# Column projections in four pieces, norm biases folded into the transposes' copies, and two norms joined in a four-layer transformer kernel

## The reference

```python
for l in range(2):                                   # first block
    h = x @ w_in[l]                                  # 13 splits: fox, mla, stick, swa
    mix = concat(fox_attention, mla, stick_breaking, sliding_window)
    x = layernorm(ALPHA * x + group_rmsnorm(mix) @ w_o[l], ln1_g[l], ln1_b[l])
    f = (silu(x @ w_gate[l]) * (x @ w_up[l])) @ w_down[l]
    x = layernorm(ALPHA * x + f, ln2_g[l], ln2_b[l])
for l in range(2):                                   # second block
    x = x + 0.5 * swiglu(rms_norm(x, ffn_norm[l, 0]), ...)
    p = rms_norm(x, mix_norm[l]) @ w_in_2[l]
    x = x + concat(dsa_attention(p), rwkv7_time_mix(p), gated_deltanet(p)) @ w_out[l]
    x = x + 0.5 * swiglu(rms_norm(x, ffn_norm[l, 1]), ...)
```

## Time and profile before

| | |
|---|---|
| median of 3 runs | 4019.3 us (4017.92 to 4021.04) |
| the profiled execution | 4015.3 us |
| its span | 4013.4 us |
| granted TensorE clock, mean | 0.945 of 2.4 GHz |
| DMA | 292.37 MB, 73 GB/s mean |

### The profile page before, as it was taken

The page is one execution under the profiler, slowest core; times in us unless marked ns, Lnnn a source line. Parts: engine busy times, 40 slices in busy tenths (PEclk is TensorE's granted clock), DMA queues, the critical chain, the costliest instruction groups (busy, mean ns, idle before and its releaser), DMA issues.

```text
span 4013.4 us, 54320 instructions
## 1 busy us (share of the span) xinstructions
PE 3754.5 (94%) x23012; PEld 3097.8 (77%) x23012; DVE 1389.5 (35%) x2950; ACT 1407.8 (35%) x2393; POOL 1340.5 (33%) x639
## 2 busy tenths in 40 slices
PE   8987999998889989999998789999999999779999
PEld 7876888887678868888766678888888866668887
DVE  2345111334531232112775741112111486662111
ACT  2443222335332233223453433223222454434221
POOL 3103444430144443444320124444444320114443
PEclk9988999998799999999997899999999997889999
DMA  4101333320123332333210023333333320003332
GB/s 120 48 14 50 100 95 97 95 64 16 38 84 95 100 108 82 97 101 93 74 32 1 3 62 97 101 96 104 97 103 95 90 58 1 2 24 93 96 96 93
DMA packets 406785, 292.37 MB, mean 73 GB/s; under 512 B 18032, under 2 KB 356880, under 8 KB 406544
## 3 DMA queue, kind: packets, MB, share of 16 engines
q1 hardware_dynamic: 400976, 284.69, 23.8%
q10 hardware_dynamic: 5136, 2.96, 0.3%
q0 software_dynamic: 432, 1.25, 0.1%
HBM read 286.77 MB, written 2.10 MB: 72 GB/s over the span
## 4 chain that ended last, share of the span: by engine, by line
PE 53%; DVE 6%; ACT 3%; issue 1%; POOL 0%; ACTq 0%; DVEq 0%
PE ps L713 8%; PE ps L715 8%; PE ps L714 8%; PE ps L797 6%; PE ps L800 6%; PE ps L799 6%; PE ps L1316 2%; PE ps L740 1%; PE ps L851 1%; PE ps L742 1%; PE ps L741 1%; PE ps L868 1%; PE ps L1105 1%; PE ps L696 1%; PE ps L859 1%
## 5 line engine op out<-in xcount | busy, mean ns | idle before, releaser
L2892 POOL TENSOR_TENSOR wl<-wraw,wh 128x1024 fp32r<-128x1024 f32 (+2 forms) x532 | 1246.3, 2343 | 2258.7 <-ACT wh L2322 2258.6
L713 PE MATMUL ps<-x_T,wh 128*128 128x512 f32 (+1 forms) x2464 | 941.1, 382 | 18.2 <-POOL wl L2892 9.0
L714 PE MATMUL ps<-x_T,wh 128*128 128x512 f32 (+1 forms) x2464 | 936.9, 380 | 0.0
L715 PE MATMUL ps<-x_T,wl 128*128 128x512 f32 (+1 forms) x2464 | 936.6, 380 | 0.0
L2322 ACT ACTIVATE wh<-wraw 128x1024 fp32r<-128x1024 f32 (+2 forms) x532 | 548.7, 1032 | 1101.8 <-PE ps L800 593.9
L713 PEld LDWEIGHTS ps<-x_T,wh 128*128 128x128 f32 x2464 | 469.0, 190 | 108.2 <-issue 15.5
L715 PEld LDWEIGHTS ps<-x_T,wl 128*128 128x128 f32 x2464 | 468.7, 190 | 86.7
L714 PEld LDWEIGHTS ps<-x_T,wh 128*128 128x128 f32 x2464 | 469.0, 190 | 85.9 <-issue 0.5
L797 PE MATMUL ps<-wh,h_T 128*128 128x512 f32 x1056 | 411.4, 390 | 0.0
L800 PE MATMUL ps<-wh,h_T 128*128 128x512 f32 x1056 | 410.9, 389 | 0.0
L799 PE MATMUL ps<-wl,h_T 128*128 128x512 f32 x1056 | 410.8, 389 | 0.0
(11 more groups left out here) (712 smaller groups left out, 5132.2 us busy)
## 6 DMA issues: line engine op xcount, KB each, us to landing
wraw<-in_ffn_w_gate_dram SPq DMA_DIRECT2D x88, 512.0 KB, 3.8
wraw<-in_ffn_w_up_dram SPq DMA_DIRECT2D x88, 512.0 KB, 3.8
wraw<-in_w_in_dram SPq DMA_DIRECT2D x82, 512.0 KB, 3.8
wraw<-in_ffn_w_down_dram SPq DMA_DIRECT2D x80, 512.0 KB, 3.7
wraw<-in_w_gate_dram SPq DMA_DIRECT2D x44, 512.0 KB, 3.8
wraw<-in_w_up_dram SPq DMA_DIRECT2D x44, 512.0 KB, 3.8
wraw<-in_w_down_dram SPq DMA_DIRECT2D x40, 512.0 KB, 3.7
wraw<-in_w_o_dram SPq DMA_DIRECT2D x16, 512.0 KB, 3.7
```

Of the source, the lines that this page charges most:

```text
L713: mm(b[:, t0:t1], wh[:, k, :], xTh[:, k, t0:t1], k == 0, False)
L714: mm(b[:, t0:t1], wh[:, k, :], xTl[:, k, t0:t1], False, False)
L715: ins = mm(b[:, t0:t1], wl[:, k, :], xTh[:, k, t0:t1], False, k == 7)
L2892: tt(wl, raw_of(w), wh.bitcast(F32), ALU.subtract).then_inc(*g.sig("w", "lo", w))
```

## The change

1. **Mixer.** A column projection is cut into four pieces of two row blocks (6 matmuls) and not three; the project lane has 53 steps for 40, the heads rounds take four of them, and gates step every fourth round.
2. **Layer norms of the first block, but the joined one.** PE transposes what DVE's gain leaves, without the bias, two token tiles to a PSUM bank (`pair_T`). The bias, now per row block of the transposed x and so a column vector, is added by ACT as the bias of the copy (`high_pair`) and by DVE in the subtraction (`low_pair`), 8 instructions of 128x256 each per pair of tiles. POOL adds the bias to `xtm` later, one half tile in each of the first eight uses of the FFN (norm 2 of layer one: two in each of the first uses of layer two). DVE takes the reciprocal of tile 3 after the low parts of tiles 0 and 1.
3. **First projections.** `first_F` transposes tiles 0 and 1 before the halves and tiles 2 and 3 behind the first; its halves (`cols_half`) do the products with the high weight part first and wait for the low part only then. Behind the norms with pairs three projections are split, not two (`halves_F`). ACT and POOL stage the weights behind in another order. Norm 2 of layer one transposes its first two tiles within the last down projection.
4. **Joined norms.** DVE adds the bias itself, the squares, mean, root and scaling of a tile run two tiles behind (`behind_norm`), and the gain of rms norm (0, 0) is the scale of `high_pair` and an operand of `low_pair`; the L1556 multiplications of that norm and the row's DMA go.
5. **DMAs on ACT's queue.** The 12 row-vector DMAs go into the second group of the preceding FFN, the small projections' matrices (`lifts`) into that of the next.
6. **Squares.** ACT's four squares of q follow `index_heads`.

```diff
@@ project_lane, mixer_rounds
-    for t in range(40):
-        if t % 3 == 0 and t:
-            work(COLS2[t // 3 - 1])
-        if t < 39:
-            piece(COLS2[t // 3], t % 3)
+    for t in range(53):
+        if t % 4 == 0 and t:
+            work(COLS2[t // 4 - 1])
+        if t < 52:
+            piece(COLS2[t // 4], t % 4)
         yield
...
-        for _ in range(3):
+        for _ in range(4):
             next(project)
...
-            elif n % 3 == 0:
+            elif n % 4 == 0:
                 next(gates)
@@ PE
-                for k in ((0, 1, 2), (3, 4, 5), (6, 7))[n]:
+                for k in (2 * n, 2 * n + 1):
...
+            def halves_F(name, n, behind):
                 two = []
-                for n in range(2):
+                for m in range(n):
                     w = use()
                     b, free = bank(("F", w), ("ev", w))
                     pe.wait_ge(*free)
                     pe.wait_ge(*at("T", "lo", name, 1, 1))
-                    pe.wait_ge(*at("w", "lo", w))
-                    cols_F(w, b, 0, 2 * P)
+                    cols_half(w, b)
                     two.append((w, b))
-                    if n == 0:
-                        to_T(name, src, ready, (3,))
+                    if m == 0:
+                        behind()
...
+            def first_F(name, src, ready, done=()):
+
+                to_T(name, src, ready, [j for j in (0, 1) if j not in done])
+                halves_F(name, 2, lambda: to_T(name, src, ready, (2, 3)))
+
+            def pair_T(name, src, ready, j):
+
+
+                p = j // 2
+                if j % 2 == 0:
+                    for m in range(4):
+                        pe.wait_ge(*bank(("T", name, p, m), ("T", "b", name, p, m))[1])
+                for m in range(4):
+                    pe.wait_ge(*at(*ready(j, m // 2)))
+                    for e_ in range(2):
+                        o = (2 * e_ + j % 2) * P
+                        ins = tr(psum[book.bank[("T", name, p, m)]][:, o:o + P],
+                                 src[:, j, (2 * m + e_) * P:(2 * m + e_ + 1) * P])
+                    if j % 2:
+                        ins.then_inc(*pe.sig("T", "t", name, p, m))
...
+                halves_F(name, 3, behind)
@@ DVE
+            def low_pair(name, p, col, op):
...
+                        ins = stt(xTl[:, k, ts_], psum_of("T", name, p, m)[:, 2 * e_ * P:2 * e_ * P + 2 * P],
+                                  col[:, k:k + 1], xTh[:, k, ts_].bitcast(F32), op, ALU.subtract)
...
                 for i in range(NT + 1):
                     if i < NT:
                         close(i)
                         stats(i, 1)
                         mean(i)
-                        inverse(i)
+                        if last or i < 3:
+                            inverse(i)
                     if i:
                         gain(i - 1)
+                    if last and i:
+                        bias(i - 1)
+                    if last and 1 < i < NT:
+                        then(i - 2)
+                    if i == 3 and not last:
+                        low_pair(*pairs, 0, *cols_)
+                        inverse(i)
+                if last:
+                    low_pair(*pairs, 0, *cols_)
+                    then(2)
+                    then(3)
+                low_pair(*pairs, 1, *cols_)
@@ ACT
+            def high_pair(name, p, bias=None, scale=None):
...
+                        if bias is not None:
+                            ins = act(dst, src, ACT.Identity, bias=bias[:, k:k + 1])
+                        else:
+                            ins = act(dst, src, ACT.Identity, scale=scale[:, k:k + 1])
...
                 for i in range(NT):
                     if i == 3:
-                        stage(wat[0] + AHEAD)
+                        stage(wat[0] + 1)
+                        if not then:
+                            high_pair(name, 0, **cols_)
...
+                    if then and i > 1:
+                        then(i - 2)
+                if then:
+                    high_pair(name, 0, **cols_)
+                    then(2)
+                    then(3)
+                stage(wat[0] + AHEAD + 1)
+                high_pair(name, 1, **cols_)
...
+                index_heads(l)
                 for j in range(NT):
                     s.wait_ge(*at("ev", w, j))
                     act(scr[j][:, :], qtm2[:, j, :], ACT.Square).then_inc(*s.sig("dsa", "sq", l, j))
-                index_heads(l)
@@ POOL
+                stage(wat[0] + AHEAD + 1)
+                bias = layer_norm(l, 0)
+                for _ in range(62):
+                    use()
+                    next(bias, None)
                 use(6, True)
-                layer_norm(l, 1)
+                stage(wat[0] + AHEAD + 1)
```

More of the change, by code:

```diff
@@ L831, in early_T, with ffn @@
                     to_T(name, src, ready, (j - 1,))
-            def ffn(n, then=None):
+            def ffn(n, then=None, done=2):
                 for grp in range(2):
                     for f in range(11):
-                        if grp or f:
-                            proj_F()
-                            proj_F()
+                        for half in range(2):
+                            if grp or 2 * f + half >= done:
+                                proj_F()
                     for half in range(2):
@@ L1569, in rms_norm, with layer_norm @@
                 for i in range(NT):
[L1570 to L1571 removed]
+                    close(i)
                     gain(i, 1)
                     mean(i)
[L1574 removed]
+                    if 0 < i < 3:
                         low(name, i - 1)
                     inverse(i)
[L1577 removed]
+                for i in range(2, NT):
                     low(name, i)
[L1580 to L1582 removed]
+            def layer_norm(l, n, close, then=None):
                 def stats(i, half):
@@ L1608, in layer_norm @@
                 last = n == 1 and l == 1
+                pairs = [("rms", 0, 0) if last else (("ln1", "ln2")[n], l)]
+                cols_ = ((colat[("ffn_norm_2", 0, 0)], ALU.mult) if last else
+                         (colat[(("ln1_b", "ln2_b")[n], l)], ALU.add))
                 for i in range(NT + 1):
@@ L1640, in close @@
                             v.wait_ge(*at("w", *(("tile", w, j) if grp and half else ("used", w))))
+                            if base and not grp:
+                                v.wait_ge(*at(*base(j, half)))
                             finish(xtm[:, j, half * 512:(half + 1) * 512], grp,
@@ L1824, in close_o @@
                 v.wait_ge(*at("w", "tile", w, j))
+                if l and not g:
+                    v.wait_ge(*at("ln", "x", 0, 1, j, half))
                 stt(xs, xs, 1.0 if g else ALPHA, psum_of("Tm", w, j)[:, :], ALU.mult, ALU.add).then_inc(
@@ L2377, in norm, with behind_norm @@
                     act(rr, rr, ACT.Sqrt, bias=eps6).then_inc(*s.sig("rms", "root", l, n, i))
-                    s.wait_ge(*at("rms", "g", l, n, i, 1))
+                    if tiled:
+                        s.wait_ge(*at("rms", "g", l, n, i, 1))
                     s.wait_ge(*at("rms", "rr", l, n, i))
-                    act(mx[:, i, :], mx[:, i, :], ACT.Identity, scale=rr).then_inc(*s.sig("rms", "x", l, n, i))
-                tiled = (l, n) != (0, 0)
+                    act(mx[:, i, :], mx[:, i, :] if tiled else xtm[:, i, :], ACT.Identity, scale=rr).then_inc(*s.sig("rms", "x", l, n, i))
+                def behind_norm(i):
+                    square(i, 0)
+                    square(i, 1)
+                    norm(i)
+                if not tiled:
+                    return behind_norm
                 for i in range(NT):
@@ L2392, in rms_norm, with layer_norm @@
                 stage(wat[0] + AHEAD)
-                for i in range(2 if tiled else 0, NT):
+                for i in range(2, NT):
                     high(name, i)
-            def layer_norm(l, n):
-                name = ("ln1", l) if n == 0 else ("ln2", l)
+            def layer_norm(l, n, then=None):
                 s.preload_act_table(ACT.Sqrt)
+                name = ("rms", 0, 0) if then else (("ln1", "ln2")[n], l)
+                cols_ = {"scale": colat[("ffn_norm_2", 0, 0)]} if then else {"bias": colat[(("ln1_b", "ln2_b")[n], l)]}
                 for i in range(NT):
                     if i == 3:
-                        stage(wat[0] + AHEAD)
+                        stage(wat[0] + 1)
+                        if not then:
+                            high_pair(name, 0, **cols_)
                     rr = sml(42 + i)
@@ L2407, in layer_norm, with ffn @@
                         scale=rr[:, 0:1]).then_inc(*s.sig("ln", "n", l, n, i))
-                if not (n == 1 and l == 1):
-                    for i in range(NT):
-                        high(name, i)
-            def ffn(n):
+                    if then and i > 1:
[6 more added lines that the diff above has]
+                high_pair(name, 1, **cols_)
```

(20 more changed lines are left out.)

117 lines of the change are left out of this document (70 added, 47 removed).

## The result

The changed kernel takes 3974.2 us (median of 4 runs, 3970.44 to 3975.54) against 4018.8: a ratio of 0.9887, 95% interval 0.9869 to 0.9904. The forecast was 3990 with a range of 3968 to 4006. The profiled execution has a span of 3972.1 us, 41.3 less than before, where the sum had 29.5.

The account below looks back on a forecast made before the run. PE, busy 94% of the span, was taken to bound the kernel, gains coming where it waits or does unneeded work. Terms -5 - 10 - 5.5 - 1 - 4 - 4 = -29.5 gave span 3985.8, median 3990; range 3968 to 4006.

Parts of the forecast that it names:

- The norms: Layer norms of the first two layers: POOL's bias leaves the chain, 2.0 at norm 1 of each layer; sum 5.
- the joined norms: Joined norms of layer two: L1556 dropped, DMAs moved, bias on DVE, squares behind each bias; gain 10, bounds 8 and 13.
- first_F: First projections behind three rms norms: two tiles transposed first, high weight part first, so PE's waits fall; 5.5 in all.
- the wait of 19.1: PE's longest single wait for the scaled tiles of an rms norm (L2380), forecast to fall to about 12.
- The term for norm 2 of layer one: Second norm of layer one: halves start at 750.8 instead of 753.48, three projections done 1.0 to 1.5 earlier; taken as 1.0.
- Squares moved: Both mixers: PE gets L2624 2.2 us sooner with the squares behind index_heads; 2.0 each, 4.0, or 0 without cover.
- Mixers: Four pieces for three: early rounds -9, then +3, -9, +4, solve tail +8; taken as -2 for each mixer, -4.
- The rounds between: Mixer rounds 32 to 49 without the chain's costly steps, estimated -9; the steps put off fall on later rounds, +4.
- (1): Rival: mixers gain fully, early rounds keep 12.3 and the tail hides, -12 each instead of -2; 3970, chance 0.13.
- (2): Rival: the norms give half, short pieces and tile 3's late chain replacing PE's waits; 10 back, 4000, chance 0.2.
- (3): Rival: a thinner mixer chain keeps the low clock 17 us longer, +15 to +17 a mixer; at +17 4028, chance 0.08.
- (4): Rival: POOL's additions hold up DVE's in the FFN by the shared port; +36 if on the path, 4026, chance 0.04.

Follow-up runs that it names:

- b_rows: The kernel before with only its 12 row DMAs moved from the joined norms into the last FFN's second group: 4016.5 us against 4018.3, ratio 0.9999.
- a_hoist: The changed kernel with ACT staging the next weight ahead of the root for k, on which it waits for DVE: 3966.7 us, ratio 0.9873.
- a_squares: The changed kernel with part 6 undone, the squares back ahead of index_heads: 3973.0 us (6 runs), ratio 0.9907.
- a_hoist_sq: The changed kernel with the next weight staged ahead of the root for k and the squares back ahead of index_heads: 3983.0 us, ratio 0.9908.
- b_pieces: The kernel before with part 1 of the change alone, the four pieces: 4000.2 us against 4017.6, ratio 0.9955.
- b_late: The kernel before, still with three pieces, with the tiles' chain held back to round 41: 3995.1 us, ratio 0.9944.
- b_first: The kernel before with the new first_F alone, at all seven places: 4029.5 us (12 runs), ratio 1.0026.
- a_three: The changed kernel with part 1 undone, the project lane back in three pieces: 4013.3 us (12 runs) against 4017.6, ratio 0.9985.
- b_squares: The kernel before with part 6 alone, the squares behind index_heads: 4043.1 us (7 runs), ratio 1.0062.

## Why the prediction was right, and where not

**The norms, the joined norms and first_F** came as computed: -2.6, -2.6 and -10.5 for -2, -2 and -10, and -5.9 for -5.5. Each was read as a chain of single instructions up to the first half projection, then as PE work; the halves started within 0.5 us of the forecast times. One sign differs: the wait of 19.1 was to fall to about 12 and is now two of 5.0 and 5.8, since PE transposes one tile between them. The term for norm 2 of layer one was too high (-0.4 for -1). b_rows shows that of the causes I listed for the joined norms one, the row DMAs, counted for nothing.

**Squares moved, -4.** Wrong in sign. The step that failed: "What is late next is the DVE chain on q, by 1.9, with about 5 us in hand before its transposes". I looked at who reads q. The one who waited first was ACT's root for k, and what stood behind it on ACT's queue was a weight. a_hoist takes the weight out of that queue and gains 8.9; a_squares and a_hoist_sq show that even so the old place is better, by 2.9 us in the first mixer with the weight hoisted, and by 3.4 and 6.4 without. In the table the two stages are 8.1 us worse than the forecast.

**Mixers, -4.** A later chain, a later end of the lane and a tail were right; the size was off. Early rounds: -7.8 for -9. Given back by round 35: about +7 for +3. Tail: +5.2 for +8. The rounds between, -9 + 4 in my sum, measured about -12. Of these 6.8 fall between the two pairs of matmuls above, where 0.50 became 1.00; for the rest the clock and the chain's missing steps aren't separated. I had used the clock row only for the rival in which it got worse, and by the sign I gave myself (wrong if the mixers' clock row differs by more than 0.1) this part of the prediction failed: the row went from 0.50 to 1.00. b_pieces and b_late show that the later chain's start brings the gain. Two smaller slips: rows 12 begin the low stretch at 2110, and it began at 2102; and the bound of +10 a mixer doesn't follow from its terms, which give 8 + 4 + 3 - 4 = 11.

**The clock elsewhere, 0.** -3.2 in the attention of layer two was in no term. b_first gains it too and b_pieces doesn't (its clock falls there to 0.51), which fits a shift of what lies ahead; no run shows what sets it off.

**Luck.** That the time came within the range owes something to errors of opposite sign: the squares were 8.1 us worse than forecast, the rest of the mixers 13.9 better, the clock elsewhere 3.2 better.

**The rivals.** (1), the mixers gaining fully, was nearest in time, 3970 against 3974.2, but not for its reason: the tail didn't hide. (2) fell: the norms gave all. (3), the low clock held longer, isn't seen in the changed kernel, whose low stretches are shorter than before, but is real: it is what three pieces do in one mixer each of b_first and a_three, for 20 us, and what a_hoist_sq shows once with four. (4) fell where I put it: every FFN is as long as before within 0.1 us. The port that I named there does hold up DVE in the heads rounds, before and after the change alike: the Trainium skill, "SBUF — State Buffer" (its section "SBUF: two separate sides"), has a DVE instruction of two SBUF operands blocked for as long as GpSimd holds the shared port, and the three rows of DVE in the changed kernel above, 2.6 to 2.8 us for 0.4 or 0.7, agree.

**Open.** What starts and ends a low stretch while PE is busy without a gap. No run here separates it; identical code had it for 0 or 7 us in one place, and the rounds of a mixer with three pieces for about 34, 41, 54, 78 or over 92.

## What to carry to other kernels

When something is moved later on one engine, follow every engine's queue behind the instruction that waits for it, the weights first, not only the tensor's readers. Read the granted clock of a stretch as a term of the sum: a stretch at 0.50 with PE "busy" cost 0.36 us for each us of it in b_first, and it can come or go without any change to the stage's own code, from one execution to the next too. So judge such a kernel by the spread of its runs and by its stages, not by one total. A chain of small dependent steps woven between other units is better started late, when there is little else left for it to thin out; one condition gave 22.5 us here.

## What the runs showed of the hardware

TensorE's clock was granted at 0.50 (1.2 GHz) for 92 us on end while PE was busy 91 of them, in a kernel (b_first) whose instructions there are those of a kernel that had it for some 41 us. It was granted at 0.50 too for 30 us in which PE did column projections and the index lane's matmuls without a gap (0.51 in a_hoist_sq, 3200 to 3230). Runs of one kernel spread over 30 to 42 us in five cases, with three pieces (b_first 4010.5 to 4043.2, b_squares 4025.3 to 4065.2, a_three 3999.1 to 4037.1) and with four (a_hoist_sq 3963.9 to 3993.7, a_squares 3964.3 to 4006.0); b_pieces, a_hoist and b_late stayed within 6.1, 1.5 and 4.3.

A VectorE addition or multiplication of two SBUF operands beside a GpSimd subtraction took 2.62 to 2.78 us, where the same instruction takes 0.42 or 0.69 alone.
